# SwiGLU's output projection as seven half-size products in an encoder kernel

## The reference, cut to what matters

```python
def encoder_layer(x, ...):
    h = rmsnorm(x, norm_mix)
    proj = jnp.einsum('btd,de->bte', h, w_in)
    ...
    x = x + jnp.einsum('bte,ed->btd', jnp.concatenate([o_gla, o_hy], axis=-1), w_out)
    h = rmsnorm(x, norm_ffn)
    ff = jax.nn.silu(h @ w_gate) * (h @ w_up)
    return x + ff @ w_down
```

## Time and profile before

| | us |
|---|---|
| median of 3 runs | 1303.85 |
| lowest and highest run | 1303.67, 1304.75 |
| profiled execution, span | 1301.7 |
| TensorE busy in it | 1265.2 (97%) |
| GpSimd busy | 667.3 (51%) |
| ScalarE busy | 530.4 (41%) |
| VectorE busy | 427.5 (33%) |

### The profile page before, as it was taken

The page is one execution under the profiler, slowest core; times in us unless marked ns, Lnnn a source line. Parts: engine busy times, 40 slices in busy tenths (PEclk is TensorE's granted clock), DMA queues, the critical chain, the costliest instruction groups (busy, mean ns, idle before and its releaser), DMA issues.

```text
span 1301.7 us, 18238 instructions
## 1 busy us (share of the span) xinstructions
PE 1265.2 (97%) x7648; PEld 1022.1 (79%) x7648; DVE 427.5 (33%) x585; ACT 530.4 (41%) x884; POOL 667.3 (51%) x395
## 2 busy tenths in 40 slices
PE   5989999999999999999999999999999999999997
PEld 4657877888888778888877777788888888888885
DVE  5865667632022220000058466663500000000003
ACT  5756655443222222211156766553522222222113
POOL 2664752564555545544436676347355555554441
PEclk9999999999999999999999999999999999999999
DMA  6221212232333223333322211222233333233322
GB/s 222 82 65 50 65 52 65 72 106 101 97 97 97 82 91 98 112 104 97 97 65 82 66 51 65 67 65 84 79 97 97 97 97 97 97 114 97 97 97 81
DMA packets 31186, 115.46 MB, mean 89 GB/s; under 512 B 3456, under 2 KB 3712, under 8 KB 30720
## 3 DMA queue, kind: packets, MB, share of 16 engines
q1 hardware_dynamic: 31104, 114.29, 27.4%
HBM read 112.18 MB, written 2.10 MB: 88 GB/s over the span
## 4 chain that ended last, share of the span: by engine, by line
PE 87%; DVE 6%; ACT 2%; issue 1%; POOL 1%; DMA 1%; SPq 0%; POOLq 0%; DVEq 0%; ACTq 0%
PE ps L1207 18%; PE ps L1209 18%; PE ps L1208 18%; PE ps L1226 6%; PE ps L1229 6%; PE ps L1227 6%; PE ps L1437 2%; PE ps L1423 2%; PE ps L1223 2%; PE ps L1218 2%; PE ps L1220 2%; POOL w_lo L779 1%; DMA w_raw<-in_units 1%; PE ps L1297 1%; PE ps L1385 1%
## 5 line engine op out<-in xcount | busy, mean ns | idle before, releaser
L779 POOL TENSOR_TENSOR w_lo<-w_raw,w_hi 128x1024 fp32r<-128x1024 f32 x192 | 465.5, 2425 | 462.1 <-ACT w_hi L447 388.7
L1207 PE MATMUL ps<-h_hi,w_hi 128*128 128x512 f32 (+1 forms) x1064 | 427.6, 402 | 2.7 <-POOL w_lo L779 1.1
L1209 PE MATMUL ps<-h_hi,w_lo 128*128 128x512 f32 (+1 forms) x1064 | 414.0, 389 | 0.0
L1208 PE MATMUL ps<-h_lo,w_hi 128*128 128x512 f32 (+1 forms) x1064 | 413.4, 389 | 0.0
L447 ACT ACTIVATE w_hi<-w_raw 128x1024 fp32r<-128x1024 f32 x192 | 201.9, 1052 | 200.7 <-PE ps L1229 194.5
L1207 PEld LDWEIGHTS ps<-h_hi,w_hi 128*128 128x128 f32 x1064 | 200.6, 189 | 54.9 <-issue 11.2
L1208 PEld LDWEIGHTS ps<-h_lo,w_hi 128*128 128x128 f32 x1064 | 200.7, 189 | 43.0 <-issue 4.3
L1209 PEld LDWEIGHTS ps<-h_hi,w_lo 128*128 128x128 f32 x1064 | 200.4, 188 | 42.2
L1181 DVE TENSOR_TENSOR hid<-ps,sg 128x512 f32<-128x512 f32 x44 | 30.4, 692 | 421.4 <-PE ps L1209 421.4
L846 POOL TENSOR_TENSOR hid_lo<-hid,hid_hi 128x512 fp32r<-128x512 f32 x44 | 56.8, 1292 | 125.9 <-ACT hid_hi L757 125.9
L757 ACT ACTIVATE hid_hi<-hid 128x512 fp32r<-128x512 f32 x44 | 27.8, 632 | 203.3 <-DVE hid L1181 203.3
(11 more groups left out here) (184 smaller groups left out, 1487.8 us busy)
## 6 DMA issues: line engine op xcount, KB each, us to landing
w_raw<-in_units SPq DMA_DIRECT2D x198, 512.0 KB, 3.6
gain<-in_gain SPq DMA_DIRECT2D x5, 512.0 KB, 4.4
par<-in_par SPq DMA_DIRECT2D x2, 1118.5 KB, 9.0
x<-in_x SPq DMA_DIRECT2D x4, 512.0 KB, 7.5
out_y<-x SPq DMA_DIRECT2D x4, 512.0 KB, 2.6
cst<-in_cst SPq DMA_DIRECT2D x1, 1024.0 KB, 13.2
cst<-in_cst SPq DMA_DIRECT2D x1, 224.0 KB, 4.0
mask_f<-in_mask SPq DMA_DIRECT2D x1, 80.0 KB, 11.4
```

The costliest lines, as they stand in the source:

```text
L779: nc.gpsimd.tensor_tensor(w_tile(g, 1), w_raw[:, g % RAW], w_tile(g, 0).bitcast(F32), ALU.subtract).then_inc(s_lo, 1)
L1207: nc.tensor.matmul(out, hi, act_hi, start=start, stop=False)
L1208: nc.tensor.matmul(out, hi, act_lo, start=False, stop=False)
L1209: return nc.tensor.matmul(out, lo, act_hi, start=False, stop=stop)
```

## The change

Down is computed by Strassen's identity on blocks of two by two. The hidden products (A) are split by tokens, first and second 256, and by the hidden width, slices 0 to 10 and 11 to 21; the weights (B) by the same halves of the contraction and by halves of the 1024 columns. In place of eight products of half-size blocks there are seven, M1 to M7, of sums of blocks. The contraction is cut into 11 pairs of slices (`PAIRS`), so that there are 77 items (product m, pair i). An item has a weight piece of 128 x 512, an activation piece of 128 x 256, two blocks of 128 tokens (j) and three matmuls each: 6 matmuls an item, 462 a layer.

The items go in two sweeps. The first has M1, M2 and M3 (33 items), the second M4 to M7 (44). The last three pairs of each sweep are done product by product.

What each engine does for them:

- SP loads for each pair three of the four blocks of weights into buffers of their own (`kept`, six pairs, during the gate and up stage; `kept_h`, five pairs, into the room of `h_hi` and `h_lo` once that stage is over), and the fourth block through three buffers (`fourth`).
- ACT rounds each weight piece (`round_item`, 128 x 512; two pieces in one instruction of 128 x 1024 where `joined` allows it) and each activation piece (128 x 256).
- POOL makes the remainders of the weight pieces of all products but M3: 66 of 77 pieces in a layer. 16 pairs of pieces are joined in layer 0, and 12 in layer 1.
- DVE makes the remainder of every activation piece (`rest_item`, 77 of 128 x 256), those of M3's weights (11 of 128 x 512), the sums of activations for the first sweep (`fourth_sum`, 22 of 128 x 256), the sums of weights and activations for the second sweep (`far_sums`, 44 of 128 x 512 and 22 of 128 x 256), and adds finished products to x (`add_product`, 28 of 128 x 512 that read PSUM). In the gate and up stage it makes one further difference (128 x 256) for each of the slices 0 to 10.
- `hid` is kept whole, in 32-bit floats, and ACT and POOL no longer round it in the gate and up stage.

The diff, cut to its core:

```diff
-UNITS = U_DOWN + FT
+UNITS = U_DOWN
+PAIRS = FT // 2
+BLOCKS, ACTS, LATE = 2 * RING, 6, 3
+FAR = (0, 1, 2, 6, 7, 8, 9, 10, 3, 4, 5)
+KEPT = 6
+FIRST = [(m, i) for i in range(PAIRS - GROUP) for m in (2, 1, 3)]
+FIRST += [(m, i) for m in (1, 2, 3) for i in range(PAIRS - GROUP, PAIRS)]
+SECOND = [(m, i) for i in FAR[:-GROUP] for m in (7, 5, 6, 4)]
+SECOND += [(m, i) for m in (5, 6, 7, 4) for i in FAR[-GROUP:]]
+EARLY = {3: 0, 5: 1, 7: 2}
...
+            def round_item(L, d):
+                m, i = ITEMS[d]
...
+                    for e in range(d, d + count):
+                        by_unit, n = held_before(L, block_at(L, e), e)
+                        act.wait_ge(s_unit if by_unit else item.sem, n)
+                    nc.scalar.activation(w_blocks(L, d, count)[0], weight_of(d, count), ACT.Copy).then_inc(s_item_hi, 1)
...
+                if d >= ACTS:
+                    act.wait_ge(item.sem, item.at(L, d - ACTS + 1))
+                nc.scalar.activation(half_hi[:, d % ACTS], hid_block(i, ACT_OF[m]), ACT.Copy).then_inc(act_hi.sem, 1)
...
-                    pool.wait_ge(hhi.sem, hhi.at(L, f + 1))
-                    nc.gpsimd.tensor_tensor(hid_lo[:, f], hid[:, f % 2], hid_hi[:, f].bitcast(F32),
-                                            ALU.subtract).then_inc(hlo.sem, 1)
-                for f in range(2, FT + 2):
-                    lo_unit(L * UNITS + U_DOWN + f)
+                for d, count in ROUNDS[L]:
+                    if d not in BY_DVE:
+                        pool.wait_ge(s_item_hi, HI_OPS[L, d])
+                        hi, lo = w_blocks(L, d, count)
+                        nc.gpsimd.tensor_tensor(lo, weight_of(d, count), hi.bitcast(F32), ALU.subtract)\
+                            .then_inc(s_item_lo, 1)
+                    if d in NEXT_HI:
+                        lo_unit((L + 1) * UNITS + NEXT_HI.index(d))
...
+            def rest_item(L, d):
+                m, i = ITEMS[d]
+                v.wait_ge(act_hi.sem, act_hi.at(L, d + 1))
+                nc.vector.tensor_tensor(half_lo[:, (d + 2) % ACTS], hid_block(i, ACT_OF[m]), half_hi[:, d % ACTS].bitcast(F32),
+                                        ALU.subtract).then_inc(act_lo.sem, 1)
+                if m == LATE:
+                    v.wait_ge(s_item_hi, HI_OPS[L, d])
+                    hi, lo = w_blocks(L, d)
+                    nc.vector.tensor_tensor(lo, weight_of(d), hi.bitcast(F32), ALU.subtract).then_inc(late_lo.sem, 1)
+            def fourth_sum(L, i):
+                to = hid_block(i, 2)
+                nc.vector.tensor_tensor(to, to, hid_block(i, 3), ALU.subtract).then_inc(fours.sem, 1)
+                v.wait_ge(fours.sem, fours.at(L, 2 * i + 1))
+                nc.vector.tensor_tensor(to, to, hid_block(i, 1), ALU.add).then_inc(fours.sem, 1)
+            def far_sums(L, k):
...
+                nc.vector.tensor_tensor(b11, b12, b11, ALU.subtract).then_inc(tw.sem, 1)
+                nc.vector.tensor_tensor(b12, b22, b12, ALU.subtract).then_inc(tw.sem, 1)
+                v.wait_ge(tw.sem, tw.at(L, 4 * k + 1))
+                nc.vector.tensor_tensor(b22, b22, b11, ALU.subtract).then_inc(tw.sem, 1)
...
+                nc.vector.tensor_tensor(s2, hid_block(i, 3), hid_block(i, 1), ALU.subtract).then_inc(twos.sem, 1)
+                nc.vector.tensor_tensor(b21, b21, b22, ALU.subtract).then_inc(tw.sem, 1)
+                nc.vector.tensor_tensor(s1, s2, s1, ALU.add).then_inc(twos.sem, 1)
...
+            def add_product(L, m, j, tt, n, done):
...
+                to = x[:, tt, half(n)]
+                last = nc.vector.tensor_tensor(to, to, ps[:, PRODUCT_BANKS[m][j], :], ALU.add)
...
+            def part(L, d, j):
...
+                pe.wait_ge(act_lo.sem, act_lo.at(L, d + 1))
+                pe.wait_ge(s_item_hi, HI_OPS[L, d])
+                nc.tensor.matmul(out, t_hi, hi, start=d == mine[0], stop=False)
+                nc.tensor.matmul(out, t_lo, hi, start=False, stop=False)
+                if m == LATE:
+                    pe.wait_ge(late_lo.sem, late_lo.at(L, i + 1))
+                else:
+                    pe.wait_ge(s_item_lo, LO_OPS[L, d])
+                return nc.tensor.matmul(out, t_hi, lo, start=False, stop=d == mine[-1])
```

More of the change, by code:

```diff
@@ L128, with block_at, held_before, halves_done @@
 PLACE = {g: i for i, g in enumerate(RINGED)}
+def block_at(L, d):
+    first = 2 * ((PLACE[L * UNITS + UNITS - 1] + 1) % RING)
+    return (first + d + (SKIPPED if d >= N_FIRST else 0)) % BLOCKS
+def held_before(L, block, d):
+    held = {}
+    for g in RINGED:
+        if g < (L + 1) * UNITS:
+            for n in range(2):
+                held[2 * (PLACE[g] % RING) + n] = (True, g + 1)
+    for e in range(d):
+        held[block_at(L, e)] = (False, L * N_ITEMS + e + 1)
+    return held[block]
+def halves_done(b):
+    if b % 2 or b == 0:
+        return [(tt, n) for tt in range(TT) for n in range(2)]
+    return [(0, 0), (1, 0), (0, 1), (1, 1), (2, 1), (3, 1), (2, 0), (3, 0)]
+def joined(L, d):
+    if d + 1 >= N_ITEMS or block_at(L, d + 1) != block_at(L, d) + 1 or ITEMS[d][1] != ITEMS[d + 1][1]:
+        return False
+    return (ITEMS[d][0], ITEMS[d + 1][0]) in ((2, 1), (6, 4))
+def roundings(L):
+    out, d = [], 0
+    while d < N_ITEMS:
+        n = 2 if joined(L, d) else 1
+        out.append((d, n))
+        d += n
+    return out
+ROUNDS = [roundings(L) for L in range(DEPTH)]
+HI_OPS = {(L, d + k): sum(len(r) for r in ROUNDS[:L]) + j + 1
+          for L in range(DEPTH) for j, (d, n) in enumerate(ROUNDS[L]) for k in range(n)}
+BY_DVE = [d for d, (m, _) in enumerate(ITEMS) if m == LATE]
+LO_OPS = {}
+for _L in range(DEPTH):
+    for _d, _n in ROUNDS[_L]:
+        if _d not in BY_DVE:
+            _j = max(LO_OPS.values(), default=0) + 1
+            LO_OPS.update({(_L, _d + _k): _j for _k in range(_n)})
 class Signal:
@@ L374, in pairs, with scaled_tile, last_half @@
                            [list(first.ap[0]), [2 * s, TOK // (2 * s)], [HEADS * TOK + s, 2], [1, s]])
+        def scaled_tile(b, tt):
+            return xs4[:, tt] if b and b % 2 == 0 else xs[:, tt % 2]
+        def last_half(b, tt):
+            return max((halves_done(b).index((tt, n)), n) for n in range(2))[1]
         def step_at(n):
@@ L403, in _ @@
             for L in range(DEPTH):
-                for n in range(UNITS):
+                for n in range(2 if L else 0, UNITS):
                     load_unit(L * UNITS + n)
@@ L1627 @@
+                if L + 1 < DEPTH:
+                    x_turn(b, 0)
+                for d in range(N_ITEMS - GROUP, N_ITEMS):
+                    last = part(L, d, 0)
+                last.then_inc(m4_first.sem, 1)
+                if L + 1 < DEPTH:
+                    x_turn(b, 1)
+                for d in range(N_ITEMS - GROUP, N_ITEMS):
+                    part(L, d, 1).then_inc(item.sem, 1)
+                if L + 1 < DEPTH:
+                    x_turn(b, 2)
 TURN_PARTS = (6.28125, 0.0019350051879882812, 3.019916050561733e-07)
```

362 lines of the change are left out of this document (264 added, 98 removed).

## The result

The changed kernel takes 1412.46 us (median of 4 runs, 1410.43 to 1413.11), against 1304.05 us for the kernel before on the same chip. The ratio is 1.083, with a 95% interval of 1.0815 to 1.0844: 8.3% slower. The forecast was 1398 us.

The account below looks back on a forecast made before the run. Down was bound by matmul count before, and by POOL's and DVE's added SBUF times after the change. Down with its start 86.8, next layer's units 4.8 and hand-over 3 make +94.6 us: 1303.85 becomes 1398, range 1345 to 1445.

Parts of the forecast that it names:

- PE's part: Down: 528 matmuls become 462 at 0.227 us each, saving 15.0 us a layer if PE never waits.
- Start of down: Down's first matmul waits for DVE's remainder of item 0: 1.25 us of idle PE in each layer.
- DVE alone: DVE's work in down by itself: 94 us a layer, with 0.345 us estimated for 256 columns; would keep pace with 104.9.
- The sum of both: In down, POOL's and DVE's SBUF-only times add because they exclude each other: 156 us a layer, 162 with exposed additions.
- Additions: Down's 28 additions of products from PSUM, 19 us a layer: a third, 6 us, taken as exposed.
- The next layer's units: Layer 0's down: POOL's two units for the next layer, formerly hidden beside PE, join the same queue: +4.8 us.
- Hand-over: Passing to layer 1, DVE's four additions and four h_lo pieces precede the third block's scaling: 0 to 5.4, 3 us taken.
- Rival A: In down, POOL and DVE work side by side and PE is the bound: 1279 us, chance 0.06.
- Rival B: In down, idle time lowers TensorE's clock too; with every item at the low level 1469 us; chance 0.08.
- Rival C: In down, exclusion is only partial for short pieces, half of DVE's time lost: 1312 us, chance 0.04.
- The lower bound: Low end for the whole kernel: DVE holds POOL up 0.54 us, additions all covered, +24.4 us a layer: 1353 us.

## Why the prediction was right, and where it was off

The time lay in the range, the direction was right, and the mechanism was the one named as deciding: POOL and DVE's SBUF-only instructions exclude each other. Three runs show it from different sides: the work of either engine made narrow brings PE back close to its pace, and moving one operand to PSUM takes 21 us out of each first sweep. By the changed kernel against the one with POOL's pieces narrow, this accounts for 58 and 55 us of down in the two layers, more than the whole loss. Point by point:

- **PE's part.** 15.0 us saved in a layer. The run with POOL's work narrow shows what is left of it: 109.1 us in layer 1, 10.7 less than before. 462 matmuls at 0.2333 us make 107.8, not 104.9. The step that took 0.227 over from the earlier trace rows was wrong by 3 us a layer. It didn't matter for the sum, as PE was not the bound.
- **Start of down.** 1.25 us. The last up product's final matmul starts at 545.78 and down's first at 547.33: 1.55 us, of which one pace of 0.23 belongs to the matmul, so PE idles for 1.3. The rest of the 1.6 us lies ahead of it.
- **DVE alone.** 0.345 us for 256 columns was an estimate; with POOL idle the four `half_lo` at 628.57 take 0.34 each from start to start.
- **The sum of both.** The prediction had 156 us of SBUF-only work in a layer, 6 us of additions, and no time in which both engines are idle. In layer 1's down one of the two is at SBUF-only work for 148.1 us, DVE makes additions alone for 6.4, and for 9.1 neither works: 163.6, where 162 was forecast. The first term is 8 us too high, the missing one 9 us, and they cancel; that the total is so close is luck. In layer 0 the same three are 154.6 (160.8 with the next layer's units), 10.2 and 8.0 us: 172.8, where 166.8 was forecast. That is 6.0 too little, but only 3.1 of it reach the table: the prediction took layer 1's 119.9 us for both layers, and the kernel before takes 122.9 in layer 0. Sweep 1 alone was put at 61.7 us and has 61.4 and 61.0 of SBUF-only work, but takes 67.4 and 67.5: additions alone take 2.6 of the difference, and for 3.4 and 3.8 us neither works, as each waits for places that PE has not freed.
- **Additions.** 12 us for the program, 13.2 by the run. But the step had them in down, and there only 4.5 us were found; the rest lies in the hand-over and at the end, where they stand in DVE's queue ahead of what everybody waits for.
- **The next layer's units.** 4.8 us, as sweep 2 of layer 0 shows (84.3 to 79.2). Moving them behind down gave the whole kernel only 2.9 us, since down's last part then takes 4.5 us longer.
- **Hand-over.** +3 us was taken out of 0 to 5.4. Without the late start of layer 1's down the stretch is some 7 us longer: PE idles for 4.62 us ahead of the third block's transposes, and the next layer's first matmuls run at half clock behind that gap, 0.21 us apart for 256 columns where full clock has 0.12. From 725.2 to 730.7 us PE is at half clock, which by these rows costs some 2.7 us (an estimate). The term was too small, and its second half, the clock, was not in it.
- **The end of the program.** Not priced, +5.8 us. It is the hand-over's queue without PE behind it: four additions, one more, the root and the scaling for the third block, then the same for the fourth. The prediction had read this queue for layer 0 and did not ask what it does in layer 1, where nothing comes after it to hide anything. With the additions narrow 5.1 of the 5.8 us go. It is more than a third of the 15 us missing; no other row of the table is off by as much.
- **Rival A** (1279 us, side by side) is refuted. Its number was too low as well: with POOL's work all but gone the kernel takes 1298.7 in its one execution. The slower pace, the start, the hand-over and the end leave about 6 us of the 30.
- **Rival B** (the clock) was given a chance of 0.08 as a whole. It happened in part: granted clock 0.82 to 0.90 in the sweeps, worth about 8 us.
- **Rival C** (half of the exclusion) is refuted by sweep 1: 61.4 and 61.0 us of SBUF-only rows, where half of DVE's time lost would leave about 44 (26.6 + 35.1 / 2, an estimate from the prediction's own terms), and by the pieces of 256 columns that end only behind a POOL piece (L1153 at 626.23).
- **The lower bound.** 1353 us leaves out the 4.8 us of the next layer's units, which the sum has; with them it would be 1358. The result doesn't hang on it.

On the Trainium skill, SBUF — State Buffer, "Who interferes with whom": the rule held for `tensor_tensor` with two SBUF inputs, both ways, and the run with the PSUM operand shows its other side, 418 ns for 128 x 256 beside a busy POOL. The Trainium skill, Advanced Engine Details and Errata, "VectorE Performance Modes", names only two-port instructions as interfering with GpSimd and gives `tensor_tensor` no such mode. If that list were complete, these instructions would not interfere; the sweeps at 67.4 and 46.3 us decide against that here.

No variant beats the kernel before by a margin worth the change. The best with all its work, everything on DVE and spread, is 2.8% slower, and even with POOL's work in down all but left out the gain is 0.4%, from one execution.

## What to carry to other kernels

Before work is put on VectorE or GpSimd because it is idle, add up the times of all GpSimd instructions and of all VectorE instructions with both inputs in SBUF over the same stretch, as if they were one engine; if the sum exceeds the bound engine's time, the sum is the new bound. VectorE instructions that read one input from PSUM were free of it here, and where both engines could do a piece, the one that needs less time should. Then follow the added instructions to the end of the program, not only through the stage they were made for: what stands ahead of the last result in a queue is paid in full.
